# Second layer of a two-layer decoder trunk: routing queries projected for three heads at a time

## What is computed

```
q = (xt @ w_q).reshape(t, PEER_HEADS, 2, PEER_HALF)          # 8 heads, 2 x 128 columns each
s = jnp.einsum("thpd,hpnd->thpn", q, sub_keys)               # 128 scores per half
s1, i1 = lax.top_k(s[:, :, 0], 16); s2, i2 = lax.top_k(s[:, :, 1], 16)
cand = (s1[..., :, None] + s2[..., None, :])                 # 256 sums, of which the best 16
...
u = jnp.take(u_tab, ic, axis=0);  a = einsum("cd,chkd->chk", xc, u)
w = gc * gelu(a)
vv = jnp.take(v_tab, ic, axis=0); out = einsum("chk,chkd->cd", w, vv)
```

## Time and profile before

| | |
|---|---|
| time, median of 3 runs | 1625.74 us (1624.55 to 1626.65) |
| the profiled execution: its own time | 1625.22 us |
| its span, first to last instruction | 1623.3 us |
| PE, DVE, POOL, ACT busy | 83%, 66%, 62%, 29% of the span |
| gathers, POOL's queue | 536.94 MB, 84.0% of the 16 engines' span |
| other loads, SP's queue | 79.26 MB, 14.7% |

### The profile page before, as it was taken

How to read it: one execution, slowest core, us unless ns; L and a number is a source line. 1 busy time by engine, 2 the same in 40 slices (tenths; PEclk the granted TensorE clock), 3 DMA queues, 4 the chain that set the end, 5 groups by cost and what they waited for, 6 DMA issues and landing times.

```text
span 1623.3 us, 17094 instructions
## 1 busy us (share of the span) xinstructions
PE 1339.6 (83%) x4558; PEld 769.0 (47%) x4558; DVE 1073.2 (66%) x2529; ACT 468.5 (29%) x1427; POOL 1013.6 (62%) x1099
## 2 busy tenths in 40 slices
PE   7999798888895899888777799989877978777775
PEld 7887544444552564354343376546444433322222
DVE  4248689988775545637787635664877977755555
ACT  0203333333332222432233221441333322211112
POOL 0006677777547655766666745675777677777774
PEclk9999999999997998899989899999988989888887
DMA  9519999999999999999999999999999999999997
GB/s 335 180 57 369 397 396 409 404 405 405 393 389 365 399 391 394 407 406 390 400 402 403 410 392 387 402 392 367 408 401 404 409 410 409 409 409 409 410 409 274
DMA packets 222153, 617.13 MB, mean 380 GB/s; under 512 B 18881, under 2 KB 88571, under 8 KB 222075
## 3 DMA queue, kind: packets, MB, share of 16 engines
q0 software_dynamic: 147456, 536.94, 84.0%
q1 hardware_dynamic: 74619, 79.26, 14.7%
HBM read 615.07 MB, written 1.05 MB: 380 GB/s over the span
## 4 chain that ended last, share of the span: by engine, by line
PE 33%; DMA 20%; POOL 15%; issue 13%; DVE 11%; ACT 6%; POOLq 0%; SPq 0%; DVEq 0%; ACTq 0%
DMA u_ring<-in_peer_u_dram,idx_now 18%; PE acc L807 16%; PE tile L777 13%; POOL v_ring L532 8%; POOL u_ring L532 7%; DVE u_ring L1022 5%; ACT diag L622 2%; ACT gelus L616 2%; DMA v_ring<-in_peer_v_dram,idx_now 2%; PE tile L909 1%; PE xf L777 1%; PE tile L904 1%; DVE xres L1049 0%; ACT pq L718 0%; PE tile L799 0%
## 5 line engine op out<-in xcount | busy, mean ns | idle before, releaser
L807 PE MATMUL acc<-v_ring,diag 128*128 128x512 f32 x1780 | 864.7, 644 | 117.7 <-ACT diag L622 64.8
L1022 DVE CUSTOM_DVE_ANT_0 u_ring<-u_ring,xf 128x1024 f32<-128x1024 f32 x512 | 613.5, 1215 | 275.3 <-DMA u_ring<-in_peer_u_dram,idx_now 273.0
L532 POOL DMA_INDIRECT v_ring<-in_peer_v_dram,idx_now x512 | 497.1, 971 | 291.8 <-PE acc L807 119.8
L807 PEld LDWEIGHTS acc<-v_ring,diag 128*128 128x128 f32 x1780 | 363.0, 209 | 589.3 <-issue 550.6
L532 POOL DMA_INDIRECT u_ring<-in_peer_u_dram,idx_now x512 | 501.2, 979 | 168.7 <-issue 138.9
L608 ACT ACTIVATE gelus<-dots 128x8 f32<-128x8 f32 x64 | 13.4, 209 | 526.4 <-DVE dots L1022 526.4
L622 ACT ACTIVATE diag<-ident,gelus 128x128 f32<-128x128 f32 x448 | 137.8, 388 | 2.1
L777 PE MATMUL tile<-w_ring,fT 128*128 128x256 f32 x480 | 110.3, 383 | 3.7 <-DVE fT L1171 3.7
L777 PEld LDWEIGHTS tile<-w_ring,fT 128*128 128x128 f32 x480 | 92.1, 193 | 27.4 <-issue 12.0
L616 ACT ACTIVATE gelus<-gelus,gates 128x1 f32<-128x1 f32 x512 | 102.1, 281 | 4.1 <-ACT gelus L608 2.3
L726 ACT ACTIVATE gexp<-best,gstat 128x16 f32<-128x16 f32 x32 | 9.8, 307 | 308.3 <-DVE best L1312 308.3
(11 more groups left out here) (170 smaller groups left out, 1046.1 us busy)
## 6 DMA issues: line engine op xcount, KB each, us to landing
w_ring<-in_peer_wq_dram SPq DMA_DIRECT2D x21, 1024.0 KB, 16.4
w_ring<-in_w_out_dram SPq DMA_DIRECT2D x12, 1024.0 KB, 24.0
w_ring<-in_w_kv_dram SPq DMA_DIRECT2D x12, 1024.0 KB, 16.5
u_ring<-in_peer_u_dram,idx_now POOLq DMA_INDIRECT x512, 10.7
v_ring<-in_peer_v_dram,idx_now POOLq DMA_INDIRECT x512, 10.6
w_ring<-in_w_in_b_dram SPq DMA_DIRECT2D x8, 1024.0 KB, 20.8
u_ring<-in_w_in_a_dram SPq DMA_DIRECT2D x4, 1024.0 KB, 12.2
w_ring<-in_w_mem_kv_dram SPq DMA_DIRECT2D x4, 1024.0 KB, 15.3
```

Of the source, the lines that this page charges most:

```text
L532: pool.indirect_dma_start(ring[:, s, :], None, rows_[:, :], bass.IndirectOffsetOnAxis(idx_now[:, column + s:column + s + 1], 0), element_o ...
L807: ins = pe.matmul(acc[:, 512 * n:512 * n + 512], diag[:, par * G + s, :], v_ring[:, s, 512 * n:512 * n + 512], start=(first and s == 0), s ...
L1022: dve.tensor_tensor_reduce(u_ring[:, s, :], u_ring[:, s, :], xf[:, :], 1.0, 0.0, ALU.mult, ALU.add, dots[:, par * G + s:par * G + s + 1])\
```

## The change

The heads of the second layer are put into lumps: heads 0 to 2, 3 to 5, and the shared pair 6 and 7. A new step `project` makes the queries of a lump: for three heads two PSUM tiles of 384 columns, for the pair one of 512. Its weights come as four pieces of 256 depths x 768 columns (rows of 3 KB, 0.75 MB) or two pieces of 512 depths x 512 columns (rows of 2 KB, 1 MB). A new helper `by_depth` on PE takes the pieces one after the other and frees each when its depths are done (the semaphore `depth_used`, on which SP then waits). ACT copies the queries into `xn`. A `route` step of phases 2 and 3 is then only the two transposes from `xn`, ACT's copy and the scores. The output rows are made in `xffn`, so that `xn` is not needed at the end.

```diff
+LUMPS = [(0, 1, 2), (3, 4, 5), tuple(SHARED)]
-    for h in range(6):
-        side[1, 9 + h] += [("route", 2, h)]
-    side[2, 8] += [("route", 2, 6)]
-    side[2, 10] += [("route", 2, 7)]
-    for g, h in zip((11, 12, 13, 14, 15), ORDER_LAST):
+    side[1, 9] += [("project", 2, 0)]
+    for g, h in zip(range(10, 16), range(6)):
+        side[1, g] += [("route", 2, h)]
+    side[1, 12] += [("project", 2, 1)]
+    side[2, 8] += [("project", 2, 2)]
+    side[2, 9][0:0] = [("route", 2, 6)]
+    side[2, 10] += [("route", 2, 7), ("project", 3, 2)]
+    for g, h in zip(range(11, 16), ORDER_LAST):
         side[2, g] += [("route", 3, h)]
-    side[3, 0] += [("route", 3, ORDER_LAST[5]), ("final", 0)]
+    side[2, 12] += [("project", 3, 0)]
+    side[2, 15] += [("project", 3, 1)]
+    side[3, 0] += [("final", 0), ("route", 3, ORDER_LAST[5])]
...
+                    before = PIECES[n - NW]
+                    if before in DEPTH_USE:
+                        sp.wait_ge(depth_used, DEPTH_USE[before] + 1)
+                    else:
+                        filled(sp, LAST_USE[before])
...
+                elif kind == "project":
+                    for key in step_tiles(step):
+                        first, count, _ = wide(key)[2:]
+                        copy_tile(key, xn[:, first:first + count], bank(key)[:, 0:count])
...
+            def by_depth(tiles, src, ready=None):
+                outs = [take(key) for key in tiles]
+                keys, width = wide(tiles[0])[0:2]
+                deep = KD // len(keys)
+                for n, at in enumerate(keys):
+                    piece_landed(pe, at)
...
+                    for t, key in zip(outs, tiles):
+                        first, count, moved = wide(key)[2:]
+                        for k in range(n * deep, n * deep + deep):
+                            if moved:
+                                ins = pe.matmul(t[:, 0:count], src(k), w[:, k - n * deep, first:first + count],
+                                                start=(k == 0), stop=(k == KD - 1))
+                                continue
...
+                    if at in DEPTH_USE and LAST_USE[at] == tiles[-1]:
+                        ins.then_inc(depth_used, 1)
...
+                        t = take(("qT", ph, h))[:, PC:2 * PC]
+                        for key in step_tiles(("project", ph, LUMP[h])):
+                            emptied(pe, key)
+                        at = PC * LUMPS[LUMP[h]].index(h)
+                        rows_ = xn[:, at:at + PC]
...
+                if step == ("norm", 1):
+                    filled(dve, ("qT", *LAST_ROUTE_EARLY))
...
-                inverse_rms(("final", c), xres[:, c, :], xn[:, :])
+                rows_ = xffn[:, c, :]
+                filled(dve, ("fT", 2 + c, 1))
+                inverse_rms(("final", c), xres[:, c, :], rows_)
```

More of the change, by code:

```diff
@@ L67 @@
 LAST_SIDES = 6
+LUMPS = [(0, 1, 2), (3, 4, 5), tuple(SHARED)]
+LUMP = {h: n for n, heads in enumerate(LUMPS) for h in heads}
 def place_of(ph, h):
@@ L155, with wide @@
 assert sorted(map(str, PE_START)) == sorted(map(str, START))
+def wide(tile):
+    kind = tile[0]
+    if kind == "Q":
+        _, ph, n, i = tile
+        width = PC * len(LUMPS[n])
+        count = 512 if width % 512 == 0 else width // 2
+        return [("wq", 2 if n == LUMP[SHARED[0]] else ph, n, d) for d in range(4 if width > 512 else 2)], width, \
+            count * i, count, True
+    return None
 def step_tiles(step):
@@ L187, in step_tiles @@
         return [("fT", step[1], i) for i in range(2)]
+    if kind == "project":
+        _, ph, n = step
+        return [("Q", ph, n, i) for i in range(2 if len(LUMPS[n]) == 3 else 1)]
     if kind == "route":
-        return [("q", *step[1:]), ("qT", *step[1:]), ("sc", *step[1:])]
+        return ([("q", *step[1:])] if step[1] < 2 else []) + [("qT", *step[1:]), ("sc", *step[1:])]
     return []
@@ L219, with pieces_of @@
 LAST_ROUTE = {ph: [r for r in ROUTES if r[0] == ph][-1] for ph in range(PHASES)}
+def pieces_of(tile):
+    if wide(tile):
+        return wide(tile)[0]
+    return [piece_of(tile)] if piece_of(tile) else []
 def piece_of(tile):
+    if wide(tile):
+        return None
     kind = tile[0]
@@ L231, in piece_of @@
     if kind == "q":
-        return (kind, 0, tile[2]) if tile[1] < 2 else (kind, 2, tile[2]) if tile[2] in SHARED else tile
+        return kind, 0, tile[2]
     if kind in ("u", "c", "b"):
@@ L240 @@
 for _t in TILES:
-    if piece_of(_t):
-        LAST_USE[piece_of(_t)] = _t
+    for _p in pieces_of(_t):
+        LAST_USE[_p] = _t
+DEPTH_USE = {}
+for _t in TILES:
+    if wide(_t) and LAST_USE[pieces_of(_t)[0]] == _t:
+        for _p in pieces_of(_t)[:-1]:
+            DEPTH_USE[_p] = len(DEPTH_USE)
 HELD = [("c", 0), ("b", 0), ("u", 1), ("c", 1), ("b", 1), ("u", 2), ("c", 2), ("b", 2)]
@@ L265, in weight_source @@
             return peer_keys[key[1]].rearrange("h t n d -> n (h t) d")
+        if kind == "wq":
+            _, _, n, d = key
+            col, width, deep = PC * LUMPS[n][0], PC * len(LUMPS[n]), 2 if len(LUMPS[n]) == 3 else 4
+            return peer_wq[1].rearrange("(k p) n -> p k n", p=P)[:, deep * d:deep * d + deep, col:col + width]
         w, col = {
@@ L376, in trunk @@
         q_copied = sem("q_copied")
+        depth_used = sem("depth_used")
         pq_made = sem("pq_made")
@@ L506, in _ @@
                 sp.wait_ge(y_final, c + 1)
[L507 removed]
+                sp.dma_start(out[0, P * c:P * c + P, :], xffn[:, c, :]).then_inc(out_stored, 16)
             sp.wait_ge(out_stored, 16 * NCH)
@@ L714, in side @@
                     n = ROUTES.index((ph, h))
-                    filled(act, ("q", ph, h))
-                    act.activation(q_rows[:, :], bank(("q", ph, h))[:, 0:PC], ACT.Copy).then_inc(q_copied, 1)
+                    if ph < 2:
+                        filled(act, ("q", ph, h))
+                        act.activation(q_rows[:, :], bank(("q", ph, h))[:, 0:PC], ACT.Copy).then_inc(q_copied, 1)
                     filled(act, ("qT", ph, h))
@@ L794, in tokens_out @@
                 done(project(t[:, 0:PC], src, lambda k: w[:, k, :]))
+            def by_depth(tiles, src, ready=None):
[4 more added lines that the diff above has]
+                    piece_landed(pe, at)
+                    if ready:
+                        ready(n)
+                    w = piece(at)[:, 0:deep * width].rearrange("p (k n) -> p k n", k=deep)
+                    for t, key in zip(outs, tiles):
[5 more added lines that the diff above has]
+                                continue
+                            for b in range(0, count, P):
+                                ins = pe.matmul(t[:, b:b + P], w[:, k - n * deep, first + b:first + b + P], src(k),
+                                                start=(k == 0 and b == 0), stop=(k == KD - 1),
+                                                skip_group_check=True)
+                        if n == len(keys) - 1:
+                            done(ins)
+                    if at in DEPTH_USE and LAST_USE[at] == tiles[-1]:
+                        ins.then_inc(depth_used, 1)
             def transposes(key, blocks):
@@ L891, in side @@
                         transposes(("fT", ph, i), [xffn[:, ph % 2, P * k:P * k + P] for k in range(4 * i, 4 * i + 4)])
+                elif kind == "project":
+                    ph = step[1]
+                    for i in range(2):
+                        emptied(pe, ("fT", ph, i))
+                    by_depth(step_tiles(step), lambda k: fT[:, ph % 2, k, :])
                 elif kind == "route":
```

30 lines of the change are left out of this document (15 added, 15 removed).

## The result

The changed kernel takes 1632.72 us (median of 6 runs, 1631.54 to 1635.57) against 1624.84 for the kernel before, measured on the same chip: the ratio is 1.0049, 95% interval 1.0039 to 1.0059. That is 7.9 us more, where the prediction had 7.5.

What follows compares the result with a forecast made beforehand. Time was taken as transferred bytes at their kind's DMA rate plus dry-queue stretches. Terms -5.4 (rows), +2.4 (1,8)/(1,9), +4.5 (2,8), +0.5 (2,12), +5.5 (2,15) sum to +7.5 us: forecast 1633.2 us, range 1622 to 1640.

Steps and rivals of the forecast that it cites:

- reserve: Gathers' time from issue to landing, guarding against a dry queue: floor 6.7 us, 10.6 around 1275 us, about 4 above.
- (2,15): Group whose projection behind the scores delays additions and POOL; no weights left to load: +5.5 us, bounds 4.3 to 7.
- Dry spells: Stretches where the DMA queue runs empty; one seen before, from 488 us while POOL stood still, lost 4.3 us.
- (2,8): Group where shorter weight loads end before POOL's gathers return, the pair's projection delaying PE: +4.5 us, bounds 2 and 6.

Runs made afterwards that it cites:

- the first experiment: Changed kernel with the projection of (2,15) put ahead of the transposes and scores, ACT's copy of the queries staying behind: 1626.98 us, ratio 1.0008 to the kernel before.
- the block of 16: Kernel before plus 16 matmuls of 384 columns, result unused, on PE behind the scores of (2,15): 1631.41 us, ratio 1.0038.

## What to carry to other kernels

Work that runs in a wait is free only in its place: moved behind the thing waited for, it delays everyone who is queued behind, and what exceeds their reserve is paid (at (2,15) 6.2 us of a block of 10.5, about 2 of one of 6.4). Before merging steps, ask on which side of the wait the merged step will stand; here the same change costs 8 us with its projections in one set of places and saves 5 with them in another. Dry spells are not independent: one that is removed can uncover the next block in line, so a single edit without effect does not clear its suspect.

## What the runs showed of the hardware that was not expected

- A DMA share near 1 is not a full rate. Behind the empty time at (2,8) the engines show shares of 0.93 to 1.00 and move 314 to 323 GB/s; with the queue full a share of 1.03 moves 410. The same packets of 4 KB take longer there on average: from 1132 to 1144 us 931 of them fill 94.7% of the 16 engines' time, so some 195 ns each, with the queue full some 164 (400 in 4 us at 1.03, from 1284 to 1288). Most take no longer (the median is 159 ns in these 12 us), a few several times as long. So a spell costs more than its empty time: of the 5.2 us about half, 2.7 us, falls into the 12 us from 1132 on. Why these packets take longer no run shows.
- The engines are nearly empty well before the last landing is seen, and stay empty after the next issue. In the changed kernel the gather that POOL issues at 1282.97 lands 9.3 us later, at 1292.3, but from 1289 on the engines move less than 140 GB/s. The next one is issued at 1293.67; no byte moves from 1292 to 1296.
- PE's clock fell in the wait. In the changed kernel PE stood idle for 5.47 us ahead of the scores of (2,15), and the granted clock from 1276 to 1280 us is 0.50, the lower of the two levels, 1.2 instead of 2.4 GHz (first row). In the first experiment, where PE projects in this wait, it stays at 1.00 (second row):

```profile
1276.00:1280.00 4.00, 2.42 (x7) 1.82 (x8) 3.93 (x8) 1.52 (x6) 3.08 (x4) 0.50 1.03 411
1276.00:1280.00 4.00, 4.00 (x13) 2.30 (x13) 3.73 (x6) 1.14 (x4) 3.06 (x4) 1.00 1.03 410
```

The 32 passes took 12.55 us in the changed kernel and 10.48 in the first experiment. This is not a new loss: before, the clock fell here too (0.89 from 1276 to 1280 us, 0.68 in the next 4 us), and the additions paid for it with 13.88 us instead of 12.18, as the prediction reckoned; in the changed kernel they take 12.18. Nor does the spell need it: the block of 16 took 10.49 us at a clock of 1.00 and cost 6.2 us.
